# Seven block products instead of eight in a feed-forward's input product, and the output product in three parts

## The chip, the core and the metric

The kernel runs on one core of one Trainium2 chip. A core has five engines with queues of their own: PE (TensorE, the matrix array), DVE (VectorE), ACT (ScalarE), POOL (GpSimd) and SP (SyncE, which here only issues DMAs). They order themselves by semaphores. The metric is the device time of one launch in microseconds (us).

## The reference, cut to what matters

Two layers of a hybrid decoder over 512 prompt tokens and 8 sample tokens (520 columns in all, stored feature-major as 128 partitions x 8 blocks x 520). Each layer has a feed-forward, a mixing stage (state-space branch, sparse attention, projections) and a second feed-forward. The diff is about the feed-forwards and the per-layer modulation that is computed beside them:

```python
D_MODEL = 1024; SEQ = 512; DEC_BATCH = 8; DEPTH = 2; D_FF = 2816

def swiglu(h, w_in, w_out):
    g, u = jnp.split(h @ w_in, 2, axis=-1)
    return (jax.nn.silu(g) * u) @ w_out

def decoder_layer(...):
    mod = jax.nn.silu(c) @ mod_w + mod_b          # 9 vectors of 1024: shift, scale, gate for 3 sub-layers
    h = modulate(rmsnorm(x, norm_pre[0]), sh0, sc0)
    x = x + 0.5 * gt0 * rmsnorm(swiglu(h, ffn1_in, ffn1_out), norm_post[0])
    ...                                            # mixing stage
    h = modulate(rmsnorm(x, norm_pre[2]), sh2, sc2)
    x = x + 0.5 * gt2 * rmsnorm(swiglu(h, ffn2_in, ffn2_out), norm_post[2])
```

All is float32.

## The kernel before, in words

**Products.** Each float32 operand is split into a high part (rounded to PE's fp32r format) and a low part (the rest), and a product is three matmuls: high x high, high x low, low x high. Tokens are the moving operand in two halves of 260 columns (`HALF`), so one 128x128 weight block costs six matmuls. A *chunk* is the weights of one output tile (8 blocks, 128x1024). SP loads it into one of four `stage` slots, ACT rounds it into `w_hi` (L916), DVE subtracts for the low part into `lo_apart` (L2025, `split`), PE multiplies (L1354). A stage slot may be loaded again when its low part is done (`lo_done`, `load`, L717); a slot of `w_hi` is free when the product four chunks back is done (`chunk_used`).

**Feed-forward.** 22 tiles of gate and 22 of up. A trip makes two hidden tiles: gate, up, gate, up (192 matmuls), each in one of four PSUM pairs. ACT takes `silu` of the gate (L999), DVE multiplies it by the up product in PSUM (`hidf`, L2168), ACT rounds the hidden tile (L1002), DVE makes its low part (L2174). The hidden tiles are made and used in two parts (12 and 10 tiles): after each, the output product runs over all 8 output tiles; ACT copies the first part's sums into `yT`, DVE adds the second's (L2198). Trips are rolled into loops on every engine (`each`, `trips`).

**Beside it.** In most trips of three of the four feed-forwards PE also computes 512 columns of the modulation (a *group*: `mod_rows` into PSUM pair 3, then ACT copies the row, L1008, and in a later place PE turns it feature-major, `turn_rows`, and DVE adds the bias, L2154). Four `mod_stage` buffers of 512 KB hold its weights. There are 32 groups beside the feed-forwards.

**The norm ahead of a feed-forward** is a chain: PE sums squares, ACT and DVE take the root, PE spreads it, DVE steps x and normalises 8 blocks (L2114 to L2125), ACT modulates (L943, L944), POOL makes `h_lo` (L2942). PE takes the blocks as they come (`tiles_together`, three chunks at once). Else POOL has no work in a feed-forward.

The order on each engine is that of the code, written out by hand.

## Time and profile before

| | us |
|---|---|
| median of 3 runs | 2919.86 (2919.12 to 2927.62) |
| profiled execution | 2926.85, span 2925.1 |
| PE busy in the span | 2817.8 (96%) |
| DVE busy | 1514.7 (52%) |
| ACT busy | 1050.1 (36%) |
| POOL busy | 361.3 (12%) |

Busy is the time in which an engine runs something. Time of the span in which PE is not busy is 107 us. The four feed-forwards end at about 472, 1487, 1907 and 2900 us, and each lasts some 385 to 420 us.

### The profile page before, as it was taken

What the parts mean: (1) busy time and instruction counts of PE and PEld (TensorE: products, weight loads), DVE (VectorE), ACT (ScalarE), POOL (GpSimd) and SP (SyncE); (2) the same over time, 40 slices, a digit from 0 to 9 for tenths busy, and PEclk for the clock granted to TensorE, in tenths of its full rate; (3) what the DMA queues carried; (4) which work ended last, traced back from release to release, by engine and by line L of the source; (5) the groups of instructions that cost most, each with busy time, mean ns of one, the idle gap of its engine ahead of it and who ended that gap; (6) DMA issues with size and microseconds to landing.
All of it is one profiled execution on the core that took longest, in us unless ns stands there. A gap on an engine that the chain in (4) does not pass through costs nothing.

```text
span 2925.1 us, 55502 instructions
## 1 busy us (share of the span) xinstructions
PE 2817.8 (96%) x22476; PEld 2613.4 (89%) x22476; DVE 1514.7 (52%) x3284; ACT 1050.1 (36%) x1881; POOL 361.3 (12%) x427
## 2 busy tenths in 40 slices
PE   6999999999999999999999999999999999999998
PEld 4999999999777799999999999989987768999997
DVE  1322247887978463222463222588777856532234
ACT  4222224545353242222242222355553523422222
POOL 3000002133043110000010000030421520100000
PEclk8999998999999999999989999999999999899998
DMA  6664434222224325445344444341222233232321
GB/s 232 200 206 126 131 111 118 88 59 66 62 67 137 116 84 170 129 130 172 92 120 135 136 124 138 90 139 52 59 59 76 81 120 113 81 96 81 98 77 65
DMA packets 450452, 324.30 MB, mean 111 GB/s; under 512 B 25113, under 2 KB 403345, under 8 KB 449498
## 3 DMA queue, kind: packets, MB, share of 16 engines
q1 hardware_dynamic: 444858, 296.60, 33.8%
q0 software_dynamic: 5408, 25.17, 2.6%
q8 instruction: 123, 2.02, 0.3%
q14 instruction: 63, 0.52, 0.1%
HBM read 310.48 MB, written 11.24 MB: 110 GB/s over the span
## 4 chain that ended last, share of the span: by engine, by line
PE 78%; DVE 14%; ACT 2%; issue 2%; DMA 2%; POOL 0%; SPq 0%; DVEq 0%; ACTq 0%; POOLq 0%
PE PS L1354 78%; DVE lo_over L2025 1%; DVE score L2559 1%; DVE best L2558 1%; DVE W L2489 1%; DVE score L2549 1%; DVE xT L2116 1%; PE PS L1588 1%; DMA stage<-in_w_in 1%; DVE counting L2296 1%; DVE tmpn L2114 1%; DMA mod_open<-in_mod_w 0%; ACT rv L1226 0%; DVE E L2242 0%; DVE cand L2242 0%
## 5 line engine op out<-in xcount | busy, mean ns | idle before, releaser
L1354 PE MATMUL PS<-h_hi,w_hi 128*128 128x260 f32 (+1 forms) x4000 | 833.7, 290 | 8.7 <-DVE lo_over L2025 5.0
L1354 PE MATMUL PS<-h_lo,w_hi 128*128 128x260 f32 (+1 forms) x4000 | 808.2, 284 | 0.0
L1354 PEld LDWEIGHTS PS<-h_hi,w_hi 128*128 128x128 f32 (+1 forms) x4000 | 618.0, 189 | 53.6 <-issue 42.3
L1354 PEld LDWEIGHTS PS<-h_lo,w_hi 128*128 128x128 f32 (+1 forms) x4000 | 619.1, 189 | 0.0
L1354 PE MATMUL PS<-h_hi,lo_apart 128*128 128x260 f32 x2816 | 567.5, 283 | 0.0
L2025 DVE TENSOR_TENSOR lo_apart<-stage,w_hi 128x1024 fp32r<-128x1024 f32 (+2 forms) x304 | 317.8, 1085 | 275.3 <-ACT w_hi L916 272.1
L1354 PEld LDWEIGHTS PS<-h_hi,lo_apart 128*128 128x128 f32 x2816 | 434.6, 189 | 0.0
L916 ACT ACTIVATE w_hi<-stage 128x1024 fp32r<-128x1024 f32 (+4 forms) x442 | 393.5, 923 | 33.4 <-DMA stage<-in_w_in 15.5
L2168 DVE TENSOR_TENSOR hidf<-sil,PS 128x520 f32<-128x520 f32 x88 | 61.3, 697 | 617.3 <-PE PS L1354 617.3
L1354 PE MATMUL PS<-hid_lo,w_hi 128*128 128x260 f32 x1408 | 283.7, 283 | 0.0
L1354 PE MATMUL PS<-hid_hi,w_hi 128*128 128x260 f32 x1408 | 283.0, 282 | 0.0
L1354 PE MATMUL PS<-hid_hi,lo_apart 128*128 128x260 f32 x1408 | 283.0, 282 | 0.0
L1354 PE MATMUL PS<-h_hi,lo_over 128*128 128x260 f32 (+1 forms) x1184 | 241.2, 286 | 0.0
L1002 ACT ACTIVATE hid_hi<-hidf 128x520 fp32r<-128x520 f32 (+1 forms) x88 | 56.2, 638 | 500.9 <-DVE hidf L2168 500.9
L2923 POOL TENSOR_TENSOR hs<-yT,r_s 128x64 f32<-128x64 f32 x6 | 1.9, 321 | 1799.7 <-ACT r_s L980 1799.7
L1354 PEld LDWEIGHTS PS<-hid_hi,lo_apart 128*128 128x128 f32 x1408 | 217.0, 188 | 0.0
L1354 PEld LDWEIGHTS PS<-hid_hi,w_hi 128*128 128x128 f32 x1408 | 216.9, 188 | 0.0
L1354 PEld LDWEIGHTS PS<-hid_lo,w_hi 128*128 128x128 f32 x1408 | 216.6, 188 | 0.0
L1354 PEld LDWEIGHTS PS<-h_hi,lo_over 128*128 128x128 f32 (+1 forms) x1184 | 184.7, 190 | 0.0
L2025 DVE TENSOR_TENSOR lo_over<-stage,w_hi 128x1024 fp32r<-128x1024 f32 (+1 forms) x138 | 147.5, 1071 | 24.3 <-ACT w_hi L916 22.7
L999 ACT ACTIVATE sil<-PS 128x520 f32<-128x520 f32 x88 | 53.2, 604 | 253.3 <-PE PS L1354 253.3
L2174 DVE TENSOR_TENSOR hid_lo<-hidf,hid_hi 128x520 fp32r<-128x520 f32 (+1 forms) x88 | 61.7, 701 | 74.8 <-ACT hid_hi L1002 74.8
(436 smaller groups left out, 3875.1 us busy)
## 6 DMA issues: line engine op xcount, KB each, us to landing
stage<-in_ffn_in SPq DMA_DIRECT2D x176, 512.0 KB, 4.8
mod_stage<-in_mod_w SPq DMA_DIRECT2D x128, 512.0 KB, 6.4
stage<-in_w_in SPq DMA_DIRECT2D x72, 512.0 KB, 3.9
stage<-in_ffn_out SPq DMA_DIRECT2D x64, 384.0 KB, 3.8
stage<-in_ffn_out SPq DMA_DIRECT2D x64, 320.0 KB, 3.4
mod_open<-in_mod_w SPq DMA_DIRECT2D x16, 512.0 KB, 9.6
stage<-in_w_out SPq DMA_DIRECT2D x16, 512.0 KB, 3.8
x_hold<-xT SPq DMA_DIRECT2D x2, 2080.0 KB, 6.5
```

Source lines behind the costliest of these rows:

```text
L916: nc.scalar.activation(w_hi[:, ch.slot, 0:ch.elems], stage[:, ch.slot, 0:ch.elems], ACT.Copy)\
L999: nc.scalar.activation(sil[:, m, :].rearrange("p (a n) -> p a n", a=2), PS[:, 2 * m, :, 0:HALF], ACT.Silu).then_inc(ev_a, 1)
L1002: nc.scalar.activation(hid_hi[:, bass.ds(i * 2 + (s.first_tile + m), 1), :], hidf[:, m:m + 1, :], ACT.Copy)\
L1354: return nc.tensor.matmul(out, lhsT, rhs, start=start, stop=stop)
L1588: return nc.tensor.transpose(out, in_, ident[p0:p0 + size, p0:p0 + size])
L2025: nc.vector.tensor_tensor(lows(ch)[:, ch.slot, 0:ch.elems], stage[:, ch.slot, 0:ch.elems], w_hi[:, ch.slot, 0:ch.elems].bitcast(FP32), ALU ...
L2114: own.step(nc.vector.scalar_tensor_tensor(tmpn[:, k % 2, 0:T], yT[:, k, 0:T], postG[:, j % 3, k, 0:1], r_wide, ALU.mult, ALU.mult))
L2116: nc.vector.tensor_tensor(xT[:, k, 0:T], xT[:, k, 0:T], tmpn[:, k % 2, 0:T], ALU.add).then_inc(x_ready, 1)
L2168: nc.vector.tensor_tensor(hidf[:, m, :].rearrange("p (a n) -> p a n", a=2), sil[:, m, :].rearrange("p (a n) -> p a n", a=2), PS[:, up, :, ...
L2174: nc.vector.tensor_tensor(hid_lo[:, f, :], hidf[:, m:m + 1, :], hid_hi[:, f, :].bitcast(FP32), ALU.subtract).then_inc(hid_lo_ready, 1)
L2296: nc.vector.tensor_scalar(counting[:], S[:], threshold, 0.0, ALU.is_ge, ALU.add, accum_out=cnt[:])\
L2489: own(nc.vector.tensor_tensor_scan(W4[:, r, q, 1:NCH + 1], V(6)[:, g:g + 1].to_broadcast([P, NCH]), W4[:, r, q, 1:NCH + 1], 0.0, ALU.mult, ...
```

## The change

The hidden tiles are now made and used in three parts (`PARTS`: 6, 8, 8). The first trip of a feed-forward stays as it was (`direct`). Each of the other ten (`win`) takes the weights of a trip as 2x2 blocks (the two halves of the inner dimension by gate and up, each block over two tiles) and the tokens as 2x2 blocks (inner halves by token halves), and makes seven block products in place of eight, by Strassen's scheme in Winograd's form. A product is 24 matmuls, so a trip has 168. For it

- POOL makes four sums of weight blocks per trip, 128x1024 each (`weight_sums`): two into new tiles, two in place in `stage`; the seven operands are split like chunks (ACT then DVE);
- all four stage slots of a trip are loaded together: slots 1 and 3 when the fifth low part of the trip before is done, slots 0 and 2 when the sixth is;
- DVE combines the products: seven additions of 128x520 that read PSUM, then the product with `silu`, in two halves. ACT takes `silu` from SBUF and copies the first product out of PSUM;
- at the start of each feed-forward DVE forms four differences of token blocks (`operand_formed`, 128x1040 each), and ACT and DVE split them; two of them lie over `xT`, which is therefore stored to DRAM first and loaded again during the last output part;
- both `split(2)` and `split(3)` of the first chunks stand ahead of the norm's second root; before, the fourth stood behind the modulation;
- the groups of the modulation stand behind the fourth and the seventh product (`mods_beside`: 14, 10 and 8 groups), and the turn of a row behind the first product of the next trip or behind the fifth;
- output chunks are whole (768 or 1024 columns for 6 or 8 blocks); DVE adds in two parts of three; nothing of the feed-forwards is rolled.

```diff
+    PARTS = (6, 8, 8)
+    OPERANDS = ('A11', 'A12', 'S3', 'S2', 'A22', 'S4', 'S1')
+        if which == 1:
+            return (l, MOD_FIRST, (2, 2, 1, 2, 1, 2, 1, 2, 1, 0)) if l == 0 else (l, 10, (1,) * 8 + (0, 0))
+        return (l + 1, 0, (1, 1, 1, 2, 1, 1, 1, 1, 1, 0)) if l < L - 1 else (l, 0, (0,) * 10)
...
+                    t.loads = {q: loaded(q) for q in (1, 3, 0, 2)}
...
+                    for q in range(4):
+                        freed[q] = ('lo', t.ring + (5 if q % 2 else 6))
...
+                def win_finished(t):
+                    hid_high(slice(t.first, t.first + 2), slice(HALF, TOK), across(hidf, 1), t.ed + 9)
+                    if 6 in t.mods:
+                        mod_row(t.mods[6][0])
...
+                def win(which, t, before):
+                    end = ffn_end(which)
+                    for j in range(7):
+                        advance(t.ring + j + 3, end)
+                        if j == 0 and before is not None and before.kind == 'win':
+                            win_finished(before)
...
+                        if j == 0:
+                            act.wait_ge(chunk_used, t.ring + 1)
+                            act.wait_ge(ev_d, t.ed - 1)
+                            nc.scalar.activation(first[:], PS[:, t.y, :, 0:HALF], ACT.Copy).then_inc(ev_a, 1)
...
+                def product(pair, ch, x_hi, x_lo):
+                    pe.wait_ge(lo_done, ch.number(1))
+                    hi, lo = highs(ch), lows(ch)
+                    for tile_ in range(2):
+                        for k in range(4):
+                            at = slice(tile_ * 512 + k * P, tile_ * 512 + (k + 1) * P)
+                            for w, x in ((hi, x_hi), (hi, x_lo), (lo, x_hi)):
+                                last = mm(PS[:, pair, tile_, 0:HALF], w[:, at], x[:, k, :],
+                                          start=(k == 0 and w is hi and x is x_hi), stop=(k == 3 and w is lo))
...
+                def turn_beside(which, m):
+                    pe.wait_ge(mod_added, m + 1)
+                    pe.wait_ge(rows_copied, m + 1)
...
+                    product(t.y, ring[t.ring], h_hi[:, 0:4, h_first], h_lo[:, 0:4, h_first])
+                    beside(0)
+                    pe.wait_ge(*evicted_before[1])
+                    product(t.x, ring[t.ring + 1], h_hi[:, 4:8, h_first], h_lo[:, 4:8, h_first])
+                    pe.wait_ge(*evicted_before[2])
+                    if t.opens:
+                        pe.wait_ge(t_lo, formed + 2)
+                    product(t.v, ring[t.ring + 2], h_hi[:, 0:4, h_second], h_lo[:, 0:4, h_second])
...
+                def weight_sums(which):
...
+                            pool.wait_ge(lo_done, t.ring)
+                            for slot in (1, 3):
+                                pool.wait_ge(stage_full[slot], t.loads[slot].arrival)
+                            pool.tensor_tensor(sum1[:], A21, A22, ALU.add).then_inc(sums_formed, 1)
+                            for slot in (0, 2):
+                                pool.wait_ge(stage_full[slot], t.loads[slot].arrival)
+                            pool.wait_ge(sums_formed, n + 1)
+                            pool.tensor_tensor(A21, A11, A21, ALU.subtract).then_inc(sums_formed, 1)
+                            pool.tensor_tensor(sum2[:], sum1[:], A11, ALU.subtract).then_inc(sums_formed, 1)
+                            pool.wait_ge(sums_formed, n + 3)
+                            pool.wait_ge(lo_done, t.ring + 2)
+                            pool.tensor_tensor(A12, A12, sum2[:], ALU.subtract).then_inc(sums_formed, 1)
```

On DVE, in a trip of the first feed-forward, the order before was this (one trip of the loop: `lo_apart` is a split, `hidf` the product with `silu`, `hid_lo` the low part of the hidden tile):

```order
L2025 TENSOR_TENSOR lo_apart<-stage,w_hi 128x1024 [waits hi_done]
L2024 REGISTER_ALU
L2025 TENSOR_TENSOR lo_apart<-stage,w_hi 128x1024 [waits hi_done]
L2165 ISA
L2166 REGISTER_ALU [waits ev_a]
L2168 TENSOR_TENSOR hidf<-sil,PS 128x520 [waits chunk_used]
L2172 REGISTER_ALU [waits ev_d]
L2174 ISA [waits hid_hi_ready]
L2174 TENSOR_TENSOR hid_lo<-hidf,hid_hi 128x520
```

That is half a trip; the other half repeats it. Now a trip of the second part is this, from its fifth product on (`sum_72` and `sum_73` are POOL's two sum tiles, `first` and `partial` hold sums of products):

```order
L2176 TENSOR_TENSOR lo_apart<-stage,w_hi 128x1024 [waits hi_done]
L2396 TENSOR_TENSOR hidf<-first,PS 128x2x260 [waits hid_lo_ready,ev_d,chunk_used]
L2399 TENSOR_TENSOR hidf<-hidf,sil 128x2x260 [waits ev_d,ev_a]
L2176 TENSOR_TENSOR lo_apart<-stage,w_hi 128x1024 [waits hi_done]
L2311 TENSOR_TENSOR modT<-PS,vecT 128x36 [waits rows_turned]
L2336 TENSOR_TENSOR hid<-hidf,hid 128x2x260 [waits hid_hi_ready]
L2401 TENSOR_TENSOR sil<-partial,PS 128x2x260 [waits chunk_used]
L2176 TENSOR_TENSOR lo_apart<-stage,w_hi 128x1024 [waits hi_done]
L2404 TENSOR_TENSOR sil<-sil,PS 128x2x260 [waits ev_d,chunk_used]
L2405 TENSOR_TENSOR hidf<-first,PS 128x2x260
L2408 TENSOR_TENSOR hidf<-hidf,sil 128x2x260 [waits ev_d,ev_a]
L2176 TENSOR_TENSOR lo_apart<-sum_73,w_hi 128x1024 [waits hi_done]
```

The three splits of `stage` here are already the next trip's A11, A12 and S3, so they wait, in order, for that trip's loads and sums, and the additions that free PSUM for PE stand behind them.

On ACT the row of the modulation was copied straight behind the hidden tile, half a trip of the first feed-forward:

```order
L913 REGISTER_ALU [waits stage_full2]
L916 ACTIVATE w_hi<-stage 128x1024 [waits chunk_used]
L913 REGISTER_ALU [waits stage_full3]
L916 ACTIVATE w_hi<-stage 128x1024 [waits chunk_used]
L997 REGISTER_ALU
L998 ISA [waits chunk_used]
L999 ACTIVATE sil<-PS 128x520 [waits ev_d]
L1001 REGISTER_ALU
L1002 ISA [waits ev_d]
L1002 ACTIVATE hid_hi<-hidf 128x520
L1006 ISA
L1008 ACTIVATE modrow<-PS 128x256 [waits rows_turned,mod_used]
```

Now, at the change from one trip to the next (second part of the same feed-forward):

```order
L992 ACTIVATE w_hi<-stage 128x1024 [waits chunk_used,sums_formed]
L1138 ACTIVATE sil<-sil 128x2x260 [waits ev_d]
L992 ACTIVATE w_hi<-sum_73 128x1024 [waits chunk_used,sums_formed]
L1090 ACTIVATE hid<-hidf 128x2x260 [waits ev_d]
L1085 ACTIVATE modrow<-PS 128x256 [waits rows_turned,mod_used]
L1136 ACTIVATE first<-PS 128x520 [waits ev_d,chunk_used]
L992 ACTIVATE w_hi<-stage 128x1024 [waits chunk_used,stage_full3,stage_full1]
```

The copy of the row now stands behind the last `silu`, a split and the rounding of the hidden half, and PE waits for it (`rows_copied`) between the first and the second product of the next trip; the split of A22 (last row) stands behind it too.

## Rows read from the trace of the kernel before

**Rows 1.** The page: busy time, granted clock by slice, the chain that ended last.
```profile
PE 2817.8 (96%) x22476; PEld 2613.4 (89%) x22476; DVE 1514.7 (52%) x3284; ACT 1050.1 (36%) x1881; POOL 361.3 (12%) x427
...
PEclk8999998999999999999989999999999999899998
...
PE 78%; DVE 14%; ACT 2%; issue 2%; DMA 2%; POOL 0%; SPq 0%; DVEq 0%; ACTq 0%; POOLq 0%
```
**Rows 2.** Windows: first feed-forward, norm behind it, last feed-forward; busy us, PEclk, DMA.
```profile
73.00:467.00 394.00, 393.38 (x3481) 377.24 (x3481) 130.49 (x187) 104.46 (x150) 0.00 (x0) 1.00 0.49 152
467.00:505.00 38.00, 35.24 (x215) 32.24 (x213) 29.07 (x51) 22.43 (x33) 13.98 (x17) 0.78 0.27 79
2536.00:2900.00 364.00, 364.00 (x3036) 364.00 (x3034) 115.07 (x132) 95.72 (x130) 0.00 (x0) 1.00 0.29 84
```
**Rows 3.** DVE in time, layer 1's last feed-forward: start, us, name, idle before.
```profile
2530.20 1.48 DVE L2025 TENSOR_TENSOR lo_apart<-stage,w_hi 128x1024 fp32r<-128x1024 f32 x1 [2.54 <-ACT w_hi L916]
2536.06 0.70 DVE L2168 TENSOR_TENSOR hidf<-sil,PS 128x520 f32<-128x520 f32 x1 [4.38 <-PE PS L1354]
2537.53 0.70 DVE L2174 TENSOR_TENSOR hid_lo<-hidf,hid_hi 128x520 fp32r<-128x520 f32 x1 [0.78 <-ACT hid_hi L1002]
2538.41 2.36 DVE L2025 TENSOR_TENSOR lo_apart<-stage,w_hi 128x1024 fp32r<-128x1024 f32 x2 [0.18 <-ACT w_hi L916]
2542.54 0.70 DVE L2168 TENSOR_TENSOR hidf<-sil,PS 128x520 f32<-128x520 f32 x1 [1.77 <-PE PS L1354]
...
2554.01 0.69 DVE L2168 TENSOR_TENSOR hidf<-sil,PS 128x520 f32<-128x520 f32 x1 [6.75 <-PE PS L1354]
```
**Rows 4.** DVE in time, first feed-forward, half trips with a group each.
```profile
103.47 0.70 DVE L2168 TENSOR_TENSOR hidf<-sil,PS 128x520 f32<-128x520 f32 x1 [8.49 <-PE PS L1354]
117.54 0.70 DVE L2168 TENSOR_TENSOR hidf<-sil,PS 128x520 f32<-128x520 f32 x1 [8.42 <-PE PS L1354]
```
**Rows 5.** Groups by form on ACT and DVE: count, busy us, mean ns.
```profile
L916 ACT ACTIVATE w_hi<-stage 128x1024 fp32r<-128x1024 f32 x264 | 268.9, 1049 | 17.4 <-DMA stage<-in_w_in 14.8 <-DMA stage<-in_ffn_in 2.1
L999 ACT ACTIVATE sil<-PS 128x520 f32<-128x520 f32 x88 | 53.2, 604 | 253.3 <-PE PS L1354 253.3
L2168 DVE TENSOR_TENSOR hidf<-sil,PS 128x520 f32<-128x520 f32 x88 | 61.3, 697 | 617.3 <-PE PS L1354 617.3
```
**Rows 6.** POOL by line: ns min/median/max, forms.
```profile
L2942 POOL TENSOR_TENSOR h_lo<-hf,h_hi x48: 1271/1292/1687, 50.1 to 2529.3; 128x512 fp32r<-128x512 f32 x48
L2973 POOL TENSOR_TENSOR CA<-C,ap x32: 620/624/1480, 521.4 to 2130.0; 128x256 f32<-128x256 f32 x32
```
**Rows 7.** DVE in time, mixing stage of layer 0, beside POOL's two W.
```profile
601.83 1.22 DVE L2025 TENSOR_TENSOR lo_over<-stage,w_hi 128x1024 fp32r<-128x1024 f32 x1
602.96 0.15 DVE L2249 SCALAR_TENSOR_TENSOR taken<-PS,bit 128x1 int32<-128x1 f32 x1
603.15 1.06 DVE L2242 TENSOR_TENSOR cand<-based,taken 128x1 int32<-128x1 int32 x1
```
**Rows 8.** POOL in the same stretch.
```profile
601.99 3.45 POOL L2996 TENSOR_TENSOR W<-mt 128x512 f32<-128x512 f32 x2 [10.97 <-DVE mt L2495]
```
**Rows 9.** DVE in time beside POOL's long row of `oh`, 844 to 870.
```profile
850.53 1.54 DVE L2025 TENSOR_TENSOR lo_over<-stage,w_hi 128x512 fp32r<-128x512 f32 x1
...
854.97 0.41 DVE L2753 SCALAR_TENSOR_TENSOR gT<-PS,gT 128x260 f32<-128x260 f32 x1
855.31 0.94 DVE L2758 SCALAR_TENSOR_TENSOR gT<-sg,gT 128x260 f32<-128x260 f32 x1
...
864.53 0.41 DVE L2758 SCALAR_TENSOR_TENSOR gT<-sg,gT 128x260 f32<-128x260 f32 x1
```
**Rows 10.** Weight loads of ffn_in, 2560 to 2640: GB/s in 40 slices.
```profile
GB/s 292 128 0 0 0 158 303 63 0 0 1 249 265 10 0 0 24 284 214 3 0 0 85 302 138 0 0 0 141 279 105 0 0 0 219 175 0 0 0 24
```
**Rows 11.** The `stage` tile, 2540 to 2640: issue to landing of one load.
```profile
DMA to landing us min/median/max: 3.1/4.0/5.6
```
**Rows 12.** The row of the modulation on ACT, all 32.
```profile
L1008 ACT ACTIVATE modrow<-PS x32: 384/384/389, 91.2 to 1802.0; 128x256 f32<-128x256 f32 x32
```
**Rows 13.** Waits of PE, first feed-forward (73 to 467): who, us, times.
```profile
PE PS L1354 <- DVE modT L2154: 0.6, 1, 0.6
```

More of the change, by code:

```diff
@@ new lines, in build, with loaded, staged @@
+    ring = []
+    plans = []
+    arrivals = [OPENED // OPEN] * 4
+    freed = [('mod', OPENED - OPEN + q + 1) for q in range(4)]
+    a = MOD_PAIRS
+    d = MOD_PAIRS
+    hid_count = win_count = mod_count = 0
+    mods_after = {}
+    def loaded(slot):
+        arrivals[slot] += 1
+        return Load(slot, 16 * arrivals[slot], freed[slot])
+    def staged(elems, in_place=False):
+        last = staged.slot
+        staged.slot = (last + 1) % 4
+        load = loaded(last)
+        ch = Chunk(len(ring), elems, 'staged', last, load.arrival, in_place)
+        ch.load = load
+        freed[last] = ('used' if in_place else 'lo', ch.base + 1)
+        ring.append(ch)
+        return ch
@@ L780, in sync @@
+                def ffn(which):
+                    for part in ffns[which]:
+                        before = None
+                        for t in part.trips:
+                            ffn_in(which, part, t, before)
+                            before = t
+                        ffn_out(which, part)
                 ffn(1)
@@ new lines, in ffn @@
+                def ffn(which, norm, gate=None):
+                    ahead[0] = ffns[which][0].trips[0].ring + 4
+                    for part in ffns[which]:
+                        before = None
+                        for t in part.trips:
+                            if t.kind == 'direct':
+                                direct(which, t)
+                            else:
+                                win(which, t, before)
+                            before = t
+                        ffn_out(which, part, norm, gate)
@@ L1573, in tensor, with ffn @@
+                def ffn(which):
+                    for part in ffns[which]:
+                        for t in part.trips:
+                            if t.kind == 'direct':
+                                direct(which, t)
+                            else:
+                                win(which, t)
+                        ffn_out(which, part)
                 if l == 0:
```

948 lines of the change are left out of this document (541 added, 407 removed).

## The prediction

> **What bounds the kernel now.** First the page's busy times and its chain that ended last: PE is busy for 96% of the span and is 78% of the chain [rows 1]. Then the windows by stage: in the last feed-forward PE is busy in every microsecond at a granted clock of 1.00 and runs 3036 matmuls in 364 us, 119.9 ns each; in the first, with the modulation beside it, 393.4 of 394 [rows 2]. PE's waits in that stretch are one of 0.6 us [rows 13]. So a feed-forward costs what its matmuls cost, and nothing else there is late. The other engines have room: DVE is busy for 115 of 364 us, ACT for 96, POOL for none [rows 2]. Last, the rhythm: two products with `silu` follow one another after 11.47 us for 96 matmuls (2542.54 to 2554.01) [rows 3], 22.94 us for a trip of 192, and after 14.07 us where a group of the modulation lies between [rows 4], so a group costs 2.6 us.
>
> **PE's work.** A trip goes from 192 to 168 matmuls. 40 trips lose 24 each, 960 x 119.9 ns = 115 us. That is the whole gain; the output products have as many matmuls as before. A trip is now worth 20.1 us of PE, 22.7 with a group, a product 2.87.
>
> **What a trip asks of DVE and POOL.** Seven splits (two follow in 2.36 us [rows 3], so 1.15 each), eleven passes over 520 elements (0.697 recorded [rows 5], some 0.63 from start to start): 8.1 + 6.9 = 15.0 us, of 20.1. POOL's four sums of 1024 elements are not in the trace. The nearest rows are its two-input forms, 1271 ns for 512 elements and 620 for 256 [rows 6]: 2.54 ns an element, 2.5 us for 1024. Below, 4 x 1.27 us would need twice the speed; above, the slowest 512 of these rows (1.69) would give 3.4 each. I take 2.5, 10 us a trip.
>
> **They exclude one another.** A split that DVE began at 601.83 took its usual 1.22 us; POOL's two W, ready at 601.99, took 3.45 instead of 2 x 1.27; then DVE's `cand`, one element from two SBUF tiles, took 1.06 us, until POOL's first W was through [rows 7, 8]. Beside POOL's `oh` a split of 512 took 1.54 us and `gT<-sg,gT` 0.94, against 0.41 for the same line when POOL paused, while `gT<-PS,gT`, with one input in PSUM, kept its 0.41 [rows 9]. So a DVE instruction with both inputs in SBUF waits for POOL's whole instruction, and POOL for it; additions from PSUM pass.
>
> The Trainium skill, "SBUF — State Buffer", section "Who interferes with whom", states this rule: the read interface is an exclusive lock, held for the whole instruction, against DVE instructions with two SBUF inputs. The trace agrees (0.94 against 0.41 us). By the rule the sum is the one below; without it, the third rival.
>
> **The loop this closes.** Splits, products with `silu` and hidden low parts have two SBUF inputs. Stage slots are single, so a trip's weights are loaded only after the low parts of the trip before. From the start of POOL's second sum (S3), in DVE's order as the change lists it: S3 holds the port 2.3; split A11 1.15; POOL's S2 2.25 (the addition from PSUM passes beside it); product with `silu` 0.6; split A12 1.15; hidden low part 0.6; S4 2.25; split S3 1.15; two additions 1.3; `silu` and product 0.7; that is 13.45. Then ACT rounds the hidden half (to 14.35), copies the first product (14.95), rounds A22 (15.95, 1.05 a split [rows 5]), and DVE splits it: 17.2 us. Now the slots are free: four loads of 512 KB. At the best slices of 284 to 303 GB/s [rows 10] 2.1 MB take 7.2 us, and a lone load lands after at least 3.1, of which 1.75 is transfer [rows 11], so 1.4 more: 8.6 us to the next S3. The loop is 25.8 us, against 20.1 of PE's and 22.9 before. Every step is charged without a gap.
>
> In it PE waits three times: product 1 for the addition behind split A11, product 2 (8.7 after S3) and product 3 (12.7) for additions that stand behind splits. From 12.7 on it is free: the trip ends 27.2 after its S3.
>
> **The four-trip parts.** POOL's sums for the first trip fall in the output product, so it runs at 20.1. S3 of the second starts at 14.3 (A22 split at 5.7, + 8.6). End: 14.3 + 2 x 25.8 + 27.2 = 93.1 us; before, 91.8.
>
> **The first part.** DVE's four differences, POOL's first three sums and the first splits all start when `h_lo` is ready and alternate: third product 4.7 us late, then the copies behind it some 3 more. I lay the two trips out at 52.5 us; before 45.9. Bounds: 45 with no exclusion, 60 if the 2 MB store of `xT` is late as well.
>
> **The modulation.** Before, 2.6 us each [rows 4]. Now the matmuls fall into PE's waits, but PE waits behind the first product for the copied row, which on ACT stands behind the last `silu`, a split and the hidden half: 14.35 + 0.38 [rows 12], then the turn, so the second product starts at 15.0 instead of 8.7. The trip ends at 32.4, not 27.2, and A22 is split 0.4 later. Within a part the loop hides the delay; at its end it shows: 5.2, and 2.4 for the group. Two groups in a trip add 1 to 4.
>
> Sum over the three parts of a feed-forward, after against before (2.57 a group):
>
> - layer 1, second (no groups): 52.5 + 93.1 + 93.1 = 238.7; 229.5: +9.2
> - layer 1, first (8): 60.2 + 101.4 + 94.0 = 255.6; 250.1: +5.5
> - layer 0, second (10): 60.2 + 101.9 + 99.4 = 261.5; 255.2: +6.3
> - layer 0, first (14): 62.8 + 105.5 + 99.9 = 268.2; 265.5: +2.7
>
> Together +24. Besides: the fourth split ahead of the root, 1.2 us in three norms, +4; the wait of the first output tile for the last hidden half (two additions, `silu`, product, rounding, low part: 4.45 us, against 2.9 or 4.3 us of matmuls that need not wait), +2; the clock, which in the norm, where PE idles for 2.8 of 38 us, is 0.78 [rows 2], and may fall to half at each opening: 2 us each, +8. Removed loop overhead is worth nothing: PE never waited on it [rows 2, 13]. That is +38 on the profiled 2926.85, 2965; this execution is 7 us above the median of 2919.86, so 2958.
>
> **The rivals.**
> - *Loop shorter than PE's trip (ends faster).* If a sum, a load or a link takes less, so that the loop is 23 and not 25.8, some 20 periods and the delays at ends and openings give back 55 to 70 us: 2890. It decides at a loop of 24. For it: additions that pass, and loads that overlap. Against it: each link above is a duration of a row. 20%.
> - *No exclusion, the gain arrives.* DVE's 15 us and POOL's 10 run side by side; the loop becomes 8.6 + 12.9 = 21.5, the trips are PE's. 115 less about 35 for openings, norms, ends and turns: 2840. Rows 7 to 9 speak against it, unless the timing of the sums falls beside PSUM additions. 10%.
> - *Nothing to tell apart.* Waits equal to the gain, within 9 us: 2920. 12%.
> - *The clock follows.* Three waits in 25 us could bring PE to half clock in each steady trip, or loads at 249 to 265 GB/s, the slower pair of those slices [rows 10], make the loop 27: 1 to 3 us more in each of 30 trips: 3020. 15%.
> - *As laid out:* 2958, between 2930 and 2990. 43%.
>
> **The numbers.** About 0.3%, 9 us, is what a measurement here can tell from no change. Faster: the first two rivals, 30%. Same: 12%. Slower: 58%. For 8 in 10 the range leaves out half of the no-exclusion case and the far end of the clock's: 2860 to 3010. The likeliest case alone: 2930 to 2990.
>
> **What would show it.** In the changed profile: PE's busy share falls to some 90%, with waits in the feed-forwards on `sil`, `hidf` and `lo_apart` of DVE, and with groups on ACT's `modrow`; S3 to S3 in a four-trip part 25 to 27 us; splits of 1024 with two modes, 1.2 and 2 to 3.5 us; POOL's sums at 2.5 and 3.5 us; slot loads of a trip landing over 8 to 9 us. It is wrong if the sums take under 2 us, if splits keep 1.2 us beside them, or if the S3 period is below 23; then PE's waits are short and the time is under 2900.

## The result, and the profile after

The changed kernel takes 2994.11 us (median of 4 runs, 2992.83 to 3001.06), the kernel before 2921.26 in the same comparison: a ratio of 1.025, with a 95% interval of 1.023 to 1.027, so 73 us slower. The forecast was 2958, slower, with a range of 2860 to 3010. Direction and mechanism are as laid out; the loss is about twice the size (73 us against 38), and the time lies 4 us above the 2930 to 2990 of the likeliest case.

The page of the changed kernel, against [rows 1]: busy times, granted clock in 40 slices, the chain by engine.

```profile
PE 2748.0 (92%) x21498; PEld 2534.2 (85%) x21498; DVE 2072.3 (69%) x3716; ACT 1205.2 (40%) x2025; POOL 802.0 (27%) x591
...
PEclk8999999999999989999999999999999999899999
...
PE 51%; DVE 26%; issue 9%; DMA 7%; ACT 5%; SPq 0%; POOL 0%; ACTq 0%; DVEq 0%; POOLq 0%
```

PE gives back 70 us of its busy time, not 115, and falls from 78% to 51% of the chain. Of the rest DVE has 26% (14% before), time named "issue" 9% (2%) and the loads 7% (2%). The windows of the last feed-forward (no groups) and of layer 1's first (eight groups), against [rows 2]: window, PE, PEld, DVE, ACT, POOL busy us, then PEclk, DMA share, GB/s.

```profile
2581.00:2967.00 386.00, 351.56 (x2797) 345.27 (x2796) 250.46 (x238) 135.12 (x167) 105.11 (x39) 0.97 0.32 85
1555.00:1961.00 406.00, 370.99 (x3077) 360.20 (x3077) 269.10 (x295) 144.42 (x184) 106.33 (x39) 0.95 0.43 127
```

2797 matmuls at 119.9 ns [rows 2] are 335 us. In the 386 us PE is idle for 34, and runs for 352: 16 us more than at full rate, at a granted clock of 0.97. Each feed-forward, from its first `silu` to the `ones,ssum` matmuls behind its output product, read in the traces of all kernels (us):

| kernel | layer 0 first (14 groups) | layer 0 second (10) | layer 1 first (8) | layer 1 second (0) |
|---|---|---|---|---|
| before | 401.9 | 391.7 | 385.7 | 364.2 |
| changed | 411.3 | 412.4 | 406.9 | 386.1 |
| `turn_later` | 400.7 | 389.6 | 389.1 | 386.0 |
| `sums_first` | 412.1 | 412.3 | 408.6 | 389.1 |
| `two_sets` | 412.3 | 415.2 | 406.4 | 358.3 |
| `narrow_sums` | 386.5 | 379.4 | 369.8 | 354.6 |
| `half_loads` | 396.8 | 401.4 | 393.4 | 365.3 |
| `sums_on_dve` | 404.0 | 398.6 | 388.7 | 370.5 |
| `three_mended` | 393.7 | 379.0 | 377.9 | 347.2 |
| `mended_half_loads` | 382.0 | 367.7 | 362.0 | 347.1 |

The change loses 9.4, 20.7, 21.2 and 21.9 us, 73 in all, so the feed-forwards hold the whole difference. (The stretch of layer 1 between its feed-forwards is 9 us shorter in this execution. It varies by 15 us over these kernels, so for a small edit the table says more than one execution's whole time. A column of the table is a single execution too: feed-forwards that an edit doesn't touch repeat within 3 us, as the first three of `two_sets` beside the changed kernel's do.)

PE's waits. Of the first feed-forward, of the second, of the last, against [rows 13]: what was waited for, us, times, longest.

```profile
PE PS L1482 <- ACT modrow L1085: 25.7, 7, 4.9
```
```profile
PE PS L1482 <- issue: 22.8, 6, 5.8
PE PS L1482 <- ACT modrow L1085: 6.8, 1, 6.8
```
```profile
PE PS L1482 <- DVE hidf L2396: 15.2, 7, 4.1
PE PS L1482 <- DVE sil L2401: 5.6, 4, 1.4
PE PS L1482 <- DVE hid L2336: 4.9, 3, 2.1
PE PS L1482 <- DVE hidf L2405: 3.9, 5, 0.8
PE PS L1482 <- DVE lo_apart L2176: 2.8, 1, 2.8
```

With groups it is the copied row, 60.0 us in 14 waits over the kernel. The 22.8 us of "issue" are the same wait under another name. In all six of them the instruction that waited is the turn of a row, here the longest, in PE's time order of the second feed-forward:

```profile
1243.00 1.01 PE L1482 MATMUL PS<-halves_sel,modrow 128*128 128x18 f32 x4 [5.81 <-issue]
```

In a second feed-forward the turn's last wait in the code is one for `vec_ready`, long past; the profile then names no releaser. In the last feed-forward it is the three additions of DVE that free PSUM, as predicted.

One period of the loop. POOL in time, layer 1's last feed-forward: start, us, name, idle before.

```profile
2689.03 2.38 POOL L3207 TENSOR_TENSOR sum<-stage 128x1024 f32<-128x1024 f32 x1 [8.13 <-DMA stage<-in_ffn_in]
2692.53 2.41 POOL L3211 TENSOR_TENSOR stage<-stage 128x1024 f32<-128x1024 f32 x1 [1.13 <-DMA stage<-in_ffn_in]
2694.90 3.38 POOL L3212 TENSOR_TENSOR sum<-sum,stage 128x1024 f32<-128x1024 f32 x1
2700.11 2.71 POOL L3215 TENSOR_TENSOR stage<-stage,sum 128x1024 f32<-128x1024 f32 x1 [1.83 <-DVE lo_apart L2176]
2716.79 2.39 POOL L3207 TENSOR_TENSOR sum<-stage 128x1024 f32<-128x1024 f32 x1 [13.97 <-DMA stage<-in_ffn_in]
2720.22 2.35 POOL L3211 TENSOR_TENSOR stage<-stage 128x1024 f32<-128x1024 f32 x1 [1.05 <-DMA stage<-in_ffn_in]
```

DVE beside it.

```profile
2693.58 2.45 DVE L2176 TENSOR_TENSOR lo_apart<-stage,w_hi 128x1024 fp32r<-128x1024 f32 x1 [5.05 <-ACT w_hi L992]
2695.95 0.68 DVE L2396 TENSOR_TENSOR hidf<-first,PS 128x520 f32<-128x520 f32 x1
2696.74 2.10 DVE L2399 TENSOR_TENSOR hidf<-hidf,sil 128x520 f32<-128x520 f32 x1
2698.76 1.21 DVE L2176 TENSOR_TENSOR lo_apart<-stage,w_hi 128x1024 fp32r<-128x1024 f32 x1
...
2701.11 2.79 DVE L2176 TENSOR_TENSOR lo_apart<-stage,w_hi 128x1024 fp32r<-128x1024 f32 x1
...
2705.22 0.70 DVE L2408 TENSOR_TENSOR hidf<-hidf,sil 128x520 f32<-128x520 f32 x1
...
2708.13 1.22 DVE L2176 TENSOR_TENSOR lo_apart<-stage,w_hi 128x1024 fp32r<-128x1024 f32 x1
...
2709.88 1.22 DVE L2176 TENSOR_TENSOR lo_apart<-stage,w_hi 128x1024 fp32r<-128x1024 f32 x1
```

Read them together, as [rows 7] and [rows 8] are read: the split of A11 begins inside POOL's second sum and takes 2.45 us instead of 1.22. POOL's third sum then takes 3.38 instead of 2.39, as it waits for that split. `hidf<-first,PS` runs beside it in its usual 0.68, and `hidf<-hidf,sil`, with both inputs in SBUF, ends 0.56 us after that sum: 2.10 instead of 0.70. The predicted order of events, counted from the second sum's start, holds link by link: the product with `silu` ends at 13.4 us (predicted 13.45), the split of A22, the row at 2708.13, at 16.8 (17.2).

What does not hold is the size of the last link, from A22's split to the next second sum. SP's queue, in time:

```profile
2709.38 5.22 SPq L783 DMA_DIRECT2D stage<-in_ffn_in  x4
```

The first loads are issued as that split ends, at 2709.35; the next second sum starts at 2720.22. The leg is 10.9 us and not 8.6; over this feed-forward it is 9.3 to 10.9. The four loads are not issued together: slots 0 and 2 hold the sum S4 until its split, one place later (the row at 2709.88, which ends 1.75 us after A22's). Here that costs nothing, as the bytes come in one stream all the same. GB/s in 40 slices and the DMA queues, 2708 to 2722, then 2854 to 2868 (another period):

```profile
GB/s 0 0 0 0 0 0 6 67 162 306 388 328 322 317 306 291 291 285 300 282 294 291 285 296 285 294 290 233 44 19 19 19 19 0 0 0 0 0 23 0
q1 hardware_dynamic: 4160, 2.10, 57.2%
q8 instruction: 1, 0.02, 0.4%
```
```profile
GB/s 0 0 0 0 0 0 0 48 123 282 304 332 347 341 306 293 293 284 291 288 291 297 287 291 293 288 293 287 132 3 0 0 0 0 0 0 0 0 0 0
q1 hardware_dynamic: 4160, 2.10, 57.2%
```

In the second of these the first load lands 3.9 us after its issue and each other one 1.7 to 1.8 us after the one before, 9.2 us in all. So the prediction's term for the start of the first load was too small: it took the least of [rows 11], 3.1, whose median is 4.0. In the first the last bytes trickle in at 19 GB/s for some 1.4 us, and a packet of the instruction queue (q8, 16 KB) lies in it. That is a pattern: in the traces of this kernel, `turn_later`, `sums_first`, `two_sets` and `narrow_sums`, four loads that are issued within 3 us have all landed after 9.9 to 10.8 us, median 10.5, in the 27 cases where such a packet starts 0.3 to 8 us after the first issue, and after 9.3 us in the median of the 57 others (two of them above 9.7). No run tests that the packet is the cause.

With groups the late freeing does count: in nine trips the second pair of loads is issued 4.9 to 6.3 us behind the first, and the leg is 10.7 to 12.5 us.

The sums by line, against [rows 6]: ns min/median/max.

```profile
L3207 POOL TENSOR_TENSOR sum<-stage x40: 2337/2396/2413, 64.0 to 2887.5; 128x1024 f32<-128x1024 f32 x40
L3212 POOL TENSOR_TENSOR sum<-sum,stage x40: 3339/3384/3417, 69.7 to 2893.5; 128x1024 f32<-128x1024 f32 x40
```

From one second sum to the next, in the four-trip parts of the last feed-forward: 21.9, 27.7 and 26.6 us, then 27.4, 26.2 and 26.3; with groups beside, 27 to 30 after the first of each part.

### The profile page after: what moved, and what is told of

It is laid out like the page before. It is cut to its first block, busy times and chain, and to the rows that moved or that the text cites. A ratio compares the mean times of both kernels' runs of the same rounds, so it can differ in the third digit from the quotient of the medians.

```text
span 2991.4 us, 52877 instructions
## 1 busy us (share of the span) xinstructions
PE 2748.0 (92%) x21498; PEld 2534.2 (85%) x21498; DVE 2072.3 (69%) x3716; ACT 1205.2 (40%) x2025; POOL 802.0 (27%) x591
## 4 chain that ended last, share of the span: by engine, by line
PE 51%; DVE 26%; issue 9%; DMA 7%; ACT 5%; SPq 0%; POOL 0%; ACTq 0%; DVEq 0%; POOLq 0%
PE PS L1482 51%; DMA stage<-in_ffn_in 5%; DVE lo_apart L2176 3%; ACT w_hi L992 3%; DVE hidf L2399 2%; DVE lo_over L2176 1%; DVE score L2801 1%; DVE best L2800 1%; DVE xT L2275 1%; DVE tmpn L2273 1%; DVE sq L2284 1%; DVE h_full L2322 1%; DVE W L2731 1%; DVE hid L2336 1%; DVE sil L2404 1%
## 5 line engine op out<-in xcount | busy, mean ns | idle before, releaser
L1482 PE MATMUL PS<-h_hi,w_hi 128*128 128x260 f32 x2720 | 702.4, 301 | 49.8 <-DVE hidf L2396 15.2
L1482 PE MATMUL PS<-h_lo,w_hi 128*128 128x260 f32 x2720 | 672.3, 290 | 0.0
L2176 DVE TENSOR_TENSOR lo_apart<-stage,w_hi 128x1024 fp32r<-128x1024 f32 (+1 forms) x312 | 482.6, 1550 | 272.1 <-ACT w_hi L992 270.6
L992 ACT ACTIVATE w_hi<-stage 128x1024 fp32r<-128x1024 f32 (+2 forms) x450 | 442.0, 990 | 482.5 <-PE PS L1482 233.7
L1482 PEld LDWEIGHTS PS<-h_hi,w_hi 128*128 128x128 f32 x2720 | 485.6, 197 | 99.4 <-issue 46.7
L1482 PEld LDWEIGHTS PS<-h_lo,w_hi 128*128 128x128 f32 x2720 | 485.7, 197 | 0.0
L1482 PE MATMUL PS<-hid,w_hi 128*128 128x260 f32 x2816 | 453.3, 283 | 8.0 <-DVE hid L2336 8.0
L1482 PEld LDWEIGHTS PS<-hid,w_hi 128*128 128x128 f32 x2816 | 385.6, 188 | 11.7 <-DVE hid L2336 9.3
L1482 PE MATMUL PS<-hid,lo_apart 128*128 128x260 f32 x1408 | 283.3, 282 | 0.0
L1482 PE MATMUL PS<-TX,w_hi 128*128 128x260 f32 x1280 | 235.2, 283 | 0.2
```

Source lines behind the costliest of these rows:

```text
L992: nc.scalar.activation(by_tile(highs(ch), ch), weights(ch), ACT.Copy).then_inc(hi_done, 1)
L1482: return nc.tensor.matmul(out, lhsT, rhs, start=start, stop=stop)
L2176: nc.vector.tensor_tensor(by_tile(lows(ch), ch), weights(ch), by_tile(highs(ch), ch).bitcast(FP32), ALU.subtract).then_inc(lo_done, 1)
```

## The experiments

The theory: two loops hold PE (a loop is a chain of waits that comes back to its start once in each trip). One goes from the load through the sums and the splits back to the stage slot; the exclusion of POOL and DVE lengthens it. The other goes through the copied row of the modulation, and is added wherever a group stands. Rivals were the loads alone, the sums alone, a stall in the output product, the clock, and the unrolling.

**`turn_later`: the turn behind the third product.**

```diff
-                        t.turns[0], pending = pending, None
+                        t.turns[2], pending = pending, None
...
                     product(t.v, ring[t.ring + 2], h_hi[:, 0:4, h_second], h_lo[:, 0:4, h_second])
+                    beside(2)
```

> The turn of a modulation row that stood behind the first product of a trip stands behind the third; all else as in the changed kernel (2994, 1.025 of before). Theory (the waits for the copied row are on the path at the ends of parts, hidden inside): PE's 60 us of waits on ACT's row copy fall below 10 us, the trips that close a part end some 5 us earlier, seven or eight of them: about 2955, 1.012. Rival 1 (those waits are the path everywhere): 60 us less, 2935, 1.005. Rival 2 (the loop of loads and sums sets every trip, the end too): the waits go over to DVE's additions, within 10 us of 2994. The last feed-forward, which has no groups, keeps its 402 us in all three.

Measured: 2950.65, ratio 1.0085 (1.0058 to 1.0112), 43 us less than the changed kernel. In the table the three feed-forwards with groups lose 10.6, 22.8 and 17.8 us, the fourth nothing. PE's waits in layer 1's first are then DVE's, the loop's own:

```profile
PE PS L1482 <- DVE hidf L2397: 7.1, 4, 2.5
PE PS L1482 <- DVE hidf L2406: 4.5, 6, 0.8
PE PS L1482 <- DVE sil L2402: 4.0, 3, 1.4
```

Of the waits for the row, 83 us (60.0 and the 22.8 named issue), the table has 51 on the path and the medians 43; the loop takes up the rest. Waits for the row of 15.0 us (three, in the first feed-forward) and 5.1 (one, in the second) stay, where below 10 were expected. The theory holds for the part ends: in the second and third feed-forward the period across each of the first two part ends falls by 6 to 7 us (62.5 to 56.3, 67.8 to 62.0; 63.3 to 56.3, 67.8 to 61.8). Part of the gain may be the clock's, as the granted clock in the second feed-forward rises from 0.95 to 0.99 when these waits go.

**`sums_first`: the output product's last copies and additions ahead of the next part's splits.**

```diff
                     for m in range(KD):
-                        advance(part.ring + m + 3, ffn_end(which))
+                        late = m >= 5 and part.index == 0
+                        if not late:
+                            advance(part.ring + m + 3, ffn_end(which))
...
+                        if late:
+                            advance(part.ring + m + 3, ffn_end(which))
```

(on ACT; on DVE the same with `part.index == 1`.)

> In the first two output products of a feed-forward the last three copies (ACT) and additions (DVE) of an output tile stand ahead of the splits of the next part's first chunks. Theory (a stall of the output product that the prediction did not have: the engines wait for the next trip's weights with PE's finished sums still in PSUM): PE's 22.8 us of waits in the second feed-forward and what corresponds in the others go: 10 to 25 us, 2970 to 2984, 1.017 to 1.022. Rival (the next trip's first split is then later by as much, and the trip ends no earlier, as the loop sets it): within 5 us of 2994.

Measured: 3002.4, ratio 1.0266 (1.0229 to 1.0303): 8 us more than the changed kernel, and no feed-forward in the table is shorter by more than 0.1. The theory falls; the time is also 3 us outside the rival's 5. PE's waits in the second feed-forward are where they were:

```profile
PE PS L1486 <- issue: 23.9, 8, 5.9
PE PS L1486 <- ACT modrow L1085: 6.6, 1, 6.6
```

The stall that this run was made for came of a misreading of "issue"; the row of the turn, above, shows what waits.

**`narrow_sums`: POOL's work cut to an eighth.**

```diff
-                            pool.tensor_tensor(sum1[:], A21, A22, ALU.add).then_inc(sums_formed, 1)
+                            c = slice(0, 512 if t.opens else 64)
+                            pool.tensor_tensor(sum1[:, :, c], A21[:, :, c], A22[:, :, c], ALU.add).then_inc(sums_formed, 1)
```

(and so for the three others. Seven eighths of each sum are left out.)

> POOL's four sums of weight blocks run over 64 of each 512 columns, but for the first such trip of each feed-forward; the rest of the sums is left out. Theory (sums and their exclusion with DVE's two-input instructions are the larger half of the loop): second sum to second sum falls from 26.6 us to 20 to 22, splits beside them keep 1.2 us, and the time falls by some 5 us in each of 30 trips and more at the ends: 2850 to 2880, 0.975 to 0.985. Rival 1 (the loads set the period): 24 us or more, 2940 to 2960. Rival 2 (clock and waits for the copied row stay): 2900 to 2920, as the first feed-forwards keep their waits.

Measured: 2867.61, ratio 0.9817 (0.978 to 0.9854), 127 us less: inside the theory's range. The sums take 0.46 us:

```profile
L3208 POOL TENSOR_TENSOR sum<-stage x40: 452/459/2401, 62.6 to 2761.7; 128x128 f32<-128x128 f32 x36, 128x1024 f32<-128x1024 f32 x4
```

Periods within the parts of the last feed-forward are 22 to 23 us, 4 less, but 26.3 where its third part opens; with groups 22 to 26, so the second rival, that clock and waits for the row keep the gain small, falls too. That a shorter loop on DVE brings the `silu` ahead of the copy earlier would explain it; it was not traced.

**`two_sets`: a second set of stage slots for every other trip, last feed-forward only.**

```diff
+    stage2 = over("stage2", [P, 4, BLK], arena0)
+    partial2 = over("partial2", [P, 2, HALF], ffn.at)
...
+                    t.other = which == 2 and l == L - 1 and trip_no % 2 == 1
```

> In the last feed-forward only, which has no groups, every second trip of seven products has its weights in a second set of four stage slots (in place of the modulation's buffers, free there); all is computed. Theory (single slots close the loop): without the load's 8 us in it the loop is gone; what stays is DVE's and POOL's time, 11 us of two-input instructions and 11 us of sums, 22 us: period 22 instead of 26.6, and the last feed-forward falls from 402 to 355 to 370 us: 2950 to 2962, 1.010 to 1.014. Rival 1 (only PE is left): period 20.1, ffn 345 us, 2937, 1.005. Rival 2 (the sums, not the loads, close it): period above 25, within 10 us of 2994.

Measured: 2968.76, ratio 1.017 (1.0131 to 1.0208), 25 us less; the range expected ended at 2962. The last feed-forward goes from 386.1 to 358.3, 28 us, 6 under before's, and its periods from the second on to 22.6, 22.6, 24.7, 22.6 and 22.6. PE's idle time in it falls from 34 to 15 us, and its busy time from 352 to 343 at a granted clock of 1.00 instead of 0.97, so some 8 of the 28 us come with the clock, which was lower where PE waited. POOL in one of them:

```profile
2692.41 3.18 POOL L3234 TENSOR_TENSOR stage<-stage 128x1024 f32<-128x1024 f32 x1 [0.17 <-POOL sum L3230]
2695.54 2.88 POOL L3235 TENSOR_TENSOR sum<-sum,stage 128x1024 f32<-128x1024 f32 x1
2699.64 2.73 POOL L3238 TENSOR_TENSOR stage<-stage,sum 128x1024 f32<-128x1024 f32 x1 [1.22 <-DVE lo_apart L2197]
2712.47 2.40 POOL L3230 TENSOR_TENSOR sum<-stage 128x1024 f32<-128x1024 f32 x1 [10.10 <-DVE lo_apart L2197]
```

With the load out of the loop, what releases POOL's first sum is DVE and no longer a DMA, and the period stays above PE's 20.1: 22 was expected, the two-input work of both engines one after the other.

**`half_loads`: 256 KB for each slot.**

```diff
-                        load(load_, rows_of(name, 0, KD, (slot % 2) * DFF + ...
+                        load(load_, rows_of(name, 0, KD if t.kind == 'direct' or t.opens else KD // 2, (slot % 2) * DFF + ...
```

> Each of a trip's four weight loads brings half of its rows (256 KB instead of 512 KB), but for the first trips of a feed-forward; the other half of each slot keeps old data, so part of the input is left out. Theory (with single slots the transfer itself is in the loop, 8.3 us of 26.6): the leg falls to 4.5 to 5.5 us, the period to 23 to 24, the time by 50 to 90 us: 2905 to 2945. Rival (the leg is the latency of one load after another, not bytes): leg above 7 us, period above 25, 2970 to 2990.

Measured: 2944.78, ratio 1.0074 (1.004 to 1.0108), 49 us less, at the small end of the theory's range. In the last feed-forward the period is 23.0 to 24.1 within parts, 27.6 where the third opens. POOL there:

```profile
2669.28 2.40 POOL L3211 TENSOR_TENSOR stage<-stage 128x1024 f32<-128x1024 f32 x1 [0.17 <-POOL sum L3207]
...
2690.06 2.40 POOL L3207 TENSOR_TENSOR sum<-stage 128x1024 f32<-128x1024 f32 x1 [10.53 <-DMA stage<-in_ffn_in]
2692.63 2.41 POOL L3211 TENSOR_TENSOR stage<-stage 128x1024 f32<-128x1024 f32 x1 [0.17 <-POOL sum L3207]
```

The second sum now waits for the first sum and not for a load. The 18.5 us from its start to the end of S4's split are as in the changed kernel, and from A22's split to the next second sum it is 6.6 us, where 4.5 to 5.5 were expected for the leg; so bytes were in the loop. With groups most periods are 27.2, PE still waits 2.8 us for the copied row in most trips, and a shorter load buys 11 to 15 us in a feed-forward, against 21 in the last.

**`sums_on_dve`: the same four sums, made by DVE.**

```diff
-                            pool.tensor_tensor(sum1[:], A21, A22, ALU.add).then_inc(sums_formed, 1)
...
+                    if ch.kind == 'A11':
...
+                        nc.vector.tensor_tensor(sum1[:], A21, A22, ALU.add).then_inc(sums_formed, 1)
...
+                        nc.vector.tensor_tensor(A21, A11, A21, ALU.subtract).then_inc(sums_formed, 1)
+                    if ch.kind == 'A12':
+                        nc.vector.tensor_tensor(sum2[:], sum1[:], A11, ALU.subtract).then_inc(sums_formed, 1)
...
+                    if ch.kind == 'A12':
...
+                        nc.vector.tensor_tensor(A12, A12, sum2[:], ALU.subtract).then_inc(sums_formed, 1)
```

> The four sums of weight blocks are made by DVE, not POOL: the first two ahead of the split of the trip's first operand, the third ahead of the second split, the fourth behind it. Theory (the exclusion between POOL and DVE and POOL's 2.4 us a sum are the larger half of the loop): a sum takes 1.2 us as a split does, no split takes over 1.3 us, from the second sum to the end of the fifth split 14 us instead of 18.5, period 22 to 23 instead of 26.6 where no group stands beside; the time falls by 50 to 100 us: 2895 to 2945, 0.99 to 1.008. Rival 1 (DVE, with 20 us of work a trip, becomes the bound and frees PSUM later): 2960 to 3000. Rival 2 (the wait for the copied row sets the trips with groups): last feed-forward 25 us and more shorter, the three others under 10 each: 2940 to 2960.

Measured: 2944.81, ratio 1.0071 (1.0044 to 1.0098), 49 us less, at the edge of the theory's range and inside that of the second rival. DVE by line: the splits from `stage` in the last feed-forward, and the first sum of each trip.

```profile
L2192 DVE TENSOR_TENSOR lo_apart<-stage,w_hi x74: 954/1220/1228, 2547.7 to 2896.1; 128x1024 fp32r<-128x1024 f32 x66, 128x768 fp32r<-128x768 f32 x8
...
L2184 DVE TENSOR_TENSOR sum<-stage x40: 1217/1219/1228, 66.2 to 2838.9; 128x1024 f32<-128x1024 f32 x40
```

No split is over 1.23 us: the slow mode is gone with POOL's sums. The period falls only to 24.5 to 26.1 in the last feed-forward (27.5 where its third part opens), as a sum now also takes 1.2 us of DVE ahead of the splits: in one period there, from the second sum to the end of A22's split is 15.2 us against 16.8, and the loads' leg stays (11.0). Size: half of what was expected of the period, which was 22 to 23. All four feed-forwards gain (7, 14, 18, 16 us), so the second rival's split of the gain is wrong.

**`three_mended`: the turn later, two sets, the sums on DVE.** The three edits above in one kernel.

> Three edits together: the turn behind the third product (alone -44 us), the second set of stage slots in the last feed-forward (alone -25), the sums on DVE. Theory (the terms are of one sum and nearly add): three feed-forwards at 22 to 24 us a trip, the last at PE's 20 to 21: 2840 to 2890, 0.973 to 0.99. Rival 1 (DVE is the bound then): no feed-forward under 22 us a trip, 2900 to 2930, 0.993 to 1.004. Rival 2 (the clock, waits at openings and ends remain as they were and weigh more): 2890 to 2910.

Measured: 2880.47, ratio 0.9838 (0.9797 to 0.988): faster than both kernels, with nothing left out. The terms 43, 25 and 49 add to 118 before rounding, and 114 came. The periods with groups are 25 to 28 us within parts, not the expected 22 to 24. The last feed-forward has one of 21.3 at a granted clock of 1.00, 1.2 above PE's 20.1; PE waits there some 0.9 us a trip for DVE's `sil`:

```profile
2509.00:2856.00 347.00, 338.34 (x2795) 335.74 (x2795) 249.48 (x276) 136.34 (x167) 0.00 (x0) 1.00 0.35 93
```

**`mended_half_loads`: that, with half of each load.**

> The three edits of before together, and the loads of a trip with half of their rows, but for the first two trips of a feed-forward (256 KB instead of 512; the other half of each slot keeps old data). Theory (in the three feed-forwards with groups the single slots' load is what is late of the last): their periods of 25 to 26 us fall to PE's 22.7, the last feed-forward, which has two sets, keeps its 347 us; 2820 to 2840. Rival 1 (another link of PE's own, from the seventh product to the next trip's first, holds them at 25): within 10 us of 2880. Rival 2 (DVE's 20 us of work and its order hold them at 24): 2845 to 2860.

Measured: 2835.45, ratio 0.97 (0.9673 to 0.9726), inside the theory's 2820 to 2840. Most periods with groups are 22.7, which is PE's own time for a trip with a group, and the last feed-forward, with its two sets, stays at 347. So halving the bytes of the single slots takes 45 us more off `three_mended` (39 of them in the three feed-forwards with groups). It leaves weights out, so it is a bound and not a kernel to use.

**`kept_busy`: PE given dummy work in its waits.**

```diff
+                    filler(4)
                     pe.wait_ge(*evicted_before[0])
...
                     beside(0)
+                    filler(5)
                     pe.wait_ge(*evicted_before[1])
...
+                    filler(3)
                     pe.wait_ge(*evicted_before[2])
```

(`filler` is `kept_running`, in the last feed-forward only.)

> In the last feed-forward, ahead of the first, second and third product of the seven trips that follow another such trip, PE runs 4, 5 and 3 extra matmuls of 512 columns into an unused PSUM bank (some 2.8 us a trip, into waits of 1 to 4 us each), so that it hardly idles. Theory (the lower clock there costs little, since the loop sets the trips): the granted clock of the last two parts goes from 0.93 and 0.98 to 1.00, but the last feed-forward, 386.1 us from its first silu to its sums, stays within 3 us. Rival (the half clock is on the path, 10 us and more of it): 376 us or less. The whole stays within 0.5% of 2994 in both.

Measured: 3003.05, ratio 1.0264. The window of the first four-trip part of the changed kernel, then of this one:

```profile
2675.00:2774.00 99.00, 88.30 (x675) 86.42 (x674) 74.45 (x68) 38.23 (x47) 37.00 (x14) 0.93 0.33 87
```
```profile
2684.00:2782.00 98.00, 93.65 (x719) 89.51 (x718) 75.34 (x67) 37.64 (x48) 39.15 (x15) 0.98 0.31 84
```

The clock rose from 0.93 to 0.98 there, not to 1.00, and the part's input product went from 99.1 to 97.2 us, the next from 96.6 to 97.0; the feed-forward has 388.4 for 386.1. But in the two output products behind them it fell from 1.00 to 0.97 and 0.96 (the windows 2782 to 2831 and 2927 to 2975), and these took 50.5 and 50.1 us for 48.1 and 48.6. Over the whole feed-forward the granted clock is 0.97 in both kernels. So the edit moved the half clock and did not remove it, and the run decides nothing about what the clock costs, there or in trips with groups.

**`before_unrolled`: the kernel before, its feed-forwards unrolled.**

```diff
-            with eng.Fori(1, n - last) as i:
-                body(i)
+            for i in range(1, n - last):
+                body(Index(i))
```

(`Index` is a plain integer; the three other loops of a feed-forward likewise.)

> The kernel before with the loops of its feed-forwards unrolled on every engine, nothing else. Theory (PE never waited for a loop's overhead, so taking it away is worth nothing): within 0.3% of before. Rival 1 (branches cost PE time between trips): 5 to 20 us faster. Rival 2 (a long straight program costs fetches): 5 us or more slower, and then part of the change's +73 us is the unrolling.

Measured: 2925.94, ratio 1.0009 (0.9991 to 1.0026), and the same four feed-forwards within 1 us (402.7, 391.7, 385.7 and 364.2). On the kernel before unrolling is worth nothing in either direction. It does change one thing, the packets of the instruction queue. The page before, then unrolled (packets, MB, share):

```profile
q8 instruction: 123, 2.02, 0.3%
```
```profile
q8 instruction: 178, 2.92, 0.4%
```

Before, PE has no wait for a load in a feed-forward and they cost nothing. In the changed kernel the loads are in the loop, and of its 15 sets of four loads issued within 3 us, five have such a packet among them and land about 1.2 us later. If that is its doing, it is some 6 us of the 73, an estimate from these landings; the changed kernel was not run rolled.

## Why the prediction was right, and what in it was mis-sized

**Right.** PE's gain (168 matmuls at 119.9 ns are 20.1 us a trip) and its loss in waits; the exclusion, and with it every link from the second sum to A22's split (16.8 us, predicted 17.2); what PE waits for; the end of a part 27.5 us after its last second sum (27.2); unrolling at nothing on the kernel before. The rival without exclusion (the second of the list, which the prediction once calls the third) had S3 periods below 23: those came only once POOL's work was cut, or loads were taken out of the loop. The rival of the shorter loop decides at 24; the changed kernel has 26 to 28.

**The load's leg: 8.6 us predicted, 9.3 to 10.9 measured without groups.** The transfer was right (7.2 us at some 290 GB/s), the start of the first load was put at 1.4 us where it is 2.1 and more, and 0.4 to 1.5 us come on top in four of nine legs of the last feed-forward, in three of them with an instruction packet. So the loop is 26.2 to 27.7 us, not 25.8. The step said "Now the slots are free: four loads of 512 KB"; two of the four are freed by the split after that one, which costs nothing there, but with groups 5 to 6 us pass between the two pairs and the leg is 10.7 to 12.5. In the last feed-forward this and the openings are 6.0 us in the first four-trip part (99.1 for 93.1) and 3.5 in the second (96.6 for 93.1).

**The opening of a part: second S3 at 14.3 us.** It is at 17.2 and 16.4. In the first trip of a part A22's split was put at 5.7 us in. It ends at 7.8 in the first four-trip part and at 5.9 in the second, and legs of 9.4 and 10.5 us follow.

**The output products.** Predicted +2 us for all; in the last feed-forward alone they take 132.7 us against 126.9. PE waits there for the last hidden half, 4.9 us in three waits, since that half now ends with DVE's chain. Over the kernel this wait is 8.0 us in six: three here, and one in each of the three others.

These three make up the last feed-forward: +9.2 predicted, +21.9 measured. They are 15 us over the sum; its first part took some 2 us less than laid out. In the others `turn_later`, with most of the row's waits gone, has -1.2, -2.1 and +3.4 us against before, where the predicted sum without its turns (three, three and two of 5.2) has -12.9, -9.3 and -4.9: 27 us more than that over the three. How these divide among the three terms and the row's waits that were left (20 us in four) was not measured.

**The copied row: 5.2 us at each of eight part ends, 42 us; "Within a part the loop hides the delay".** It came to 51 in the table and 43 in the medians, as `turn_later` shows. The waits inside parts, most of them 3.4 to 4.9 us, are hidden only in part: with `turn_later` the periods there go from 1 us more to 3 us less. That the row closes a loop of its own of 27.2 us is argued from `half_loads`, where most periods with groups stay at 27.2 with shorter loads; which of its links make the 27.2 is open.

**Terms that did not come.** The fourth split ahead of the norm's root was priced at 4 us; the one norm between two feed-forwards took 34.5 us before (last sums to next `silu`), 32.7 after and 34.4 in `half_loads`, which has the same norm. The clock at openings, 8 us, was not found as such. But the clock does follow the waits: it is granted at 0.97, 0.95, 0.95 and 0.97 in the four feed-forwards, 1.00 before, and PE's busy time beyond full rate is 16 us in the last. So the rival of the clock is borne out as to what happens; what it costs stays open, since `kept_busy` did not take it away. The 12 us of these two terms are in the forecast's 38, so the terms that did come were forecast at 26 us of the 73.

**Where the 115 us are.** With every loop mended (`mended_half_loads`) the four feed-forwards are 19.9, 24.0, 23.7 and 17.1 us shorter than before, 85 in all. Of the remaining 30 the last feed-forward has some 12: about 5 in its first part, where two trips take 45 us for PE's 40, 2.5 in each four-trip part (83.2 for 80.6), and 2 in the output products. In the others the first period of a feed-forward is still 28.3 to 33.6 us; their rest was not taken apart. So the scheme's gain is real on PE, and was lost to a loop of single slots, POOL's sums and their exclusion with DVE, and beside it to the row.

## What to carry to other kernels

Saving PE work pays only as far as the engines that feed it keep pace: sum for each a whole loop, from the load through every user of a buffer back to the load, and ask of each slot which instruction frees it last. Work put on an idle engine isn't free where it blocks another's instructions: the four sums cost less on the busier DVE (4 x 1.2 us) than on idle POOL (4 x 2.4, some 4 us more in blocked instructions of DVE, and 1.3 in POOL's own waits), 49 us in all here. A row of another computation that PE must wait for belongs where its copy is already done; moving it by two products was worth 43 us.

## What the runs showed of the hardware

- An instruction of DVE with two SBUF inputs that begins inside one of POOL's takes as long as POOL's rest and its own: splits of 1024 have modes of 1.22, 2.45, 2.8 and 3.43 us, and POOL's sums of 2.39, 2.71 and 3.38. Additions with one input in PSUM keep 0.68 beside a sum. Without POOL's sums all 94 splits of the last feed-forward are at or under 1.23. This is the exclusive lock of the Trainium skill, "SBUF — State Buffer", section "Who interferes with whom". The trace agrees, and both sides pay for it.
- A sum of two 128x1024 tiles takes 2.39 us on POOL and 1.22 on DVE, also in place, a factor of 1.96. The Trainium skill, "GPSIMD Engine Reference", section "4.1 Engine selection", gives elementwise work to VectorE, with GpSimd about twice as slow for two inputs: the trace agrees.
- Four loads of 512 KB issued within 3 us come as one stream of some 290 GB/s: they land 1.7 to 1.8 us apart, the first 3.9 us after its issue, the last 9.2 to 9.4 after it. A later issue of the second pair, by 1.7 us, costs nothing; by 5 to 6 us it does (legs of 10.7 to 12.5).
- Where a 16 KB packet of the instruction queue falls among such loads, the last lands about 1.2 us later (median 10.5 us in 27 cases, 9.3 in 57 others). A cause is not shown. The unrolled feed-forwards have 178 such packets for 123.
- "issue" as a releaser can hide a real wait: where an instruction waits for several semaphores and the last by the order of the code had long come, the profile may name none: 22.8 us in six waits of PE here. The instruction itself told what it was.
